# Gate projection of layers one and two as one rounded product over 80 stacked partitions

## The reference, cut to what matters

```python
h = x @ w_in                                   # (256, 2048) @ (2048, IN_WIDTH)
a_q, a_k, a_v, a_z, b_q, b_k, b_v, b_z, b_lr, m_q, m_z = jnp.split(h, cuts, axis=-1)
gate_logit = (b_lr @ gate_w + gate_b)          # b_lr: 256 x 16, gate_w: 16 x 256, per layer
log_g = jax.nn.log_sigmoid(gate_logit) / GATE_TAU
o_b = gla_chunk_recurrence(b_q, b_k, b_v, log_g)
```

## Time and profile before

| what | value |
|---|---|
| median of three executions | 2252.95 us (2252.88 to 2253.16) |
| span of the profiled execution | 2251.9 us |
| TensorE busy | 2240.0 us, 99% |
| TensorE weight loads | 2014.9 us, 89% |
| VectorE, ScalarE, GpSimd busy | 1555.0, 1296.2, 12.8 us |
| DMA | 460.04 MB, mean 204 GB/s |

### The profile page before, as it was taken

How to read it: one execution, slowest core, us unless ns; L and a number is a source line. 1 busy time by engine, 2 the same in 40 slices (tenths; PEclk the granted TensorE clock), 3 DMA queues, 4 the chain that set the end, 5 groups by cost and what they waited for, 6 DMA issues and landing times.

```text
span 2251.9 us, 35137 instructions
## 1 busy us (share of the span) xinstructions
PE 2240.0 (99%) x14045; PEld 2014.9 (89%) x14045; DVE 1555.0 (69%) x1772; ACT 1296.2 (58%) x1740; POOL 12.8 (1%) x18
## 2 busy tenths in 40 slices
PE   9999999999999999999999999999999999999998
PEld 8899998888999988888999999988999999998887
DVE  6576577775765777788787577866766666665555
ACT  6555576454555764666765467555655556554444
POOL 0000000000000000000000000000000000000000
PEclk9999999999999999999999999999999999999999
DMA  9655557676555684656565556675666666666664
GB/s 333 209 165 169 178 179 281 233 236 197 169 155 187 193 295 151 225 189 190 183 196 191 187 169 198 210 283 196 198 205 200 197 204 205 198 225 241 203 203 146
DMA packets 130532, 460.04 MB, mean 204 GB/s; under 512 B 13848, under 2 KB 20544, under 8 KB 128448
## 3 DMA queue, kind: packets, MB, share of 16 engines
q1 hardware_dynamic: 129376, 451.43, 60.8%
q0 software_dynamic: 848, 6.30, 0.8%
q10 hardware_dynamic: 144, 0.07, 0.0%
HBM read 449.35 MB, written 8.40 MB: 203 GB/s over the span
## 4 chain that ended last, share of the span: by engine, by line
PE 96%; DVE 2%; ACT 1%; DMA 1%; issue 0%; SPq 0%; DVEq 0%; ACTq 0%
PE banks L317 91%; PE banks L417 1%; PE banks L402 1%; PE banks L448 1%; PE banks L381 1%; PE banks L409 1%; DMA w_bc<-in_norm_mix_post 0%; DVE wl L652 0%; ACT wh L485 0%; DMA early<-in_kv_t 0%; PE banks L461 0%; PE banks L463 0%; PE banks L462 0%; DVE lacc L813 0%; PE banks L425 0%
## 5 line engine op out<-in xcount | busy, mean ns | idle before, releaser
L652 DVE TENSOR_TENSOR wl<-raw,wh 128x1024 fp32r<-128x1024 f32 x774 | 940.6, 1223 | 484.4 <-ACT wh L485 479.9
L485 ACT ACTIVATE wh<-raw 128x1024 fp32r<-128x1024 f32 (+1 forms) x777 | 813.2, 1052 | 494.5 <-PE banks L317 423.9
L317 PE MATMUL banks<-xx,wh 128*128 128x512 f32 (+1 forms) x3760 | 857.7, 380 | 0.0
L317 PEld LDWEIGHTS banks<-xx,wh 128*128 128x128 f32 (+1 forms) x3760 | 688.9, 189 | 91.6 <-issue 1.0
L317 PEld LDWEIGHTS banks<-xx,wl 128*128 128x128 f32 x3712 | 455.2, 192 | 13.5
L317 PE MATMUL banks<-xx,wl 128*128 128x256 f32 x3712 | 464.3, 276 | 0.0
L317 PE MATMUL banks<-wh,xx 128*128 128x512 f32 x1504 | 360.2, 380 | 0.0
L317 PEld LDWEIGHTS banks<-wh,xx 128*128 128x128 f32 x1504 | 282.9, 189 | 39.3
L317 PE MATMUL banks<-wl,xx 128*128 128x512 f32 x752 | 196.1, 379 | 0.0
L317 PEld LDWEIGHTS banks<-wl,xx 128*128 128x128 f32 x752 | 142.2, 189 | 20.1
L317 PE MATMUL banks<-wh,yy 128*128 128x512 f32 x416 | 98.4, 379 | 0.0
(11 more groups left out here) (287 smaller groups left out, 1762.7 us busy)
## 6 DMA issues: line engine op xcount, KB each, us to landing
raw<-in_w_in_f SPq DMA_DIRECT2D x304, 512.0 KB, 3.6
raw<-in_w_ffn_f SPq DMA_DIRECT2D x160, 512.0 KB, 4.0
raw<-in_w_ffn_down SPq DMA_DIRECT2D x88, 512.0 KB, 4.3
raw<-in_w_in_t SPq DMA_DIRECT2D x80, 512.0 KB, 3.6
raw<-in_w_out_t SPq DMA_DIRECT2D x64, 512.0 KB, 4.7
raw<-in_w_o_t SPq DMA_DIRECT2D x32, 512.0 KB, 4.7
raw<-in_kv_f SPq DMA_DIRECT2D x16, 512.0 KB, 3.9
raw<-in_w_up_a_f SPq DMA_DIRECT2D x16, 512.0 KB, 3.5
```

The lines of the kernel that those rows point to most:

```text
L317: return self.e.matmul(bank, stationary, moving, start=start, stop=stop, skip_group_check=True)
L485: self.e.activation(hi, source, ACT.Copy).then_inc(done.sem, 1)
L652: self.e.tensor_tensor(lo, source, hi.bitcast(f32), ALU.subtract).then_inc(done.sem, 1)
```

## The change

The gate projection is no longer a product of plain fp32. Weights and sums are split in a rounded part and a rest, and the parts are stacked on partitions, so that one rounded product of 80 rows and 256 columns gives, for each half, rounded times rounded, rest times rounded and rounded times rest. Rows 16 to 31 and 48 to 63 are zero.

The weights come in by one load of a table `gate_rows` (80 x 512), in which the weights of both layers stand three times, at partitions 0, 32 and 64, with zeros between. ScalarE rounds all 80 rows into `gw` and VectorE puts the rest into partitions 64 to 79, once. In each layer GpSimd clears `blr[0:80]`, then ScalarE writes the rounded sums to partitions 0 to 15 and 64 to 79 and VectorE the rest to 32 to 47. The sum itself now goes to a scratch `total`.

```diff
-        gw = sb("gw", 512)
+        gw = sb("gw", 512, f32r)
...
-                    i = self.e.matmul(banks[4][:, t * S:(t + 1) * S], gw[0:16, c:c + P], blr[0:16, :], start=True, stop=True)
+                    i = self.e.matmul(banks[4][:, t * S:(t + 1) * S], gw[0:80, c:c + P], blr[0:80, :], start=True, stop=True)
...
+            def gate_weights(self, graw, loaded, hi_done, lo_done):          # ScalarE
+                self.wait_ge(loaded)
+                self.e.activation(gw[0:80, :], graw[0:80, :], ACT.Copy).then_inc(hi_done.sem, 1)
+
+            def stack_gates(self, blr, total, made, cleared, free, hi_done, lo_done):
+                self.wait_ge(made, cleared, *free)
+                self.e.activation(blr[0:16, :], total, ACT.Copy).then_inc(hi_done[0].sem, 1)
+                self.e.activation(blr[64:80, :], total, ACT.Copy).then_inc(hi_done[1].sem, 1)
...
+            def gate_weights(self, graw, loaded, hi_done, lo_done):          # VectorE
+                self.wait_ge(hi_done)
+                self.e.tensor_tensor(gw[64:80, :], graw[64:80, :], gw[64:80, :].bitcast(f32), ALU.subtract).then_inc(lo_done.sem, 1)
+
+            def stack_gates(self, blr, total, made, cleared, free, hi_done, lo_done):
+                self.wait_ge(hi_done[0], cleared)
+                self.e.tensor_tensor(blr[32:48, :], total, blr[0:16, :].bitcast(f32), ALU.subtract).then_inc(lo_done.sem, 1)
...
+            def clear_gates(self, blr, free, done):                          # GpSimd
+                self.wait_ge(*free)
+                self.e.memset(blr[0:80, :].bitcast(f32), 0.0).then_inc(done.sem, 1)
...
-            t_gw = [load((l_gw0, l_gw1)[l_], gw[0:16, 256 * l_:256 * l_ + 256], A["b_gate_w"][l_]) for l_ in range(2)]
+            graw = at("graw", 104, 512)
+            t_gw = load(l_gw, graw[0:80, :], A["gate_rows"])
...
                 b, tok = narrow_f(X, free=x_ready)
-                c1 = narrow_sum(b, tok, 16, blr[0:16, :], tb[0:16, 0:S], fence + gate_free["t"])
+                total = tb[0:16, S:2 * S]
+                c1 = narrow_sum(b, tok, 16, total, tb[0:16, 0:S], fence + gate_free["t"])
+                cleared = after(sums_cleared)
+                x.clear_gates(blr, fence, cleared)
+                if l_ == 0:
+                    gates_hi, gates_lo = after(gates_rounded), after(gates_left)
+                    x.gate_weights(graw, t_gw, gates_hi, gates_lo)
+                sums_hi, sums_lo = afters(sums_rounded, 2), after(sums_left)
+                x.stack_gates(blr, total, c1, cleared, fence, sums_hi, sums_lo)
...
-                    made, free = (c1, t_gw[l_]), bank_free[4]
+                    made, free = (gates_hi, gates_lo, *sums_hi, sums_lo), bank_free[4]
```

More of the change, by code:

```diff
@@ L183 @@
         differences_across = evacuate = exact = exp_of_minus = exp_of_minus_abs = exps = first_product = \
-        forget_exps = forget_gates = forget_sum = gate_by = gate_half = gate_sum = gate_y = hi_features = \
+        forget_exps = forget_gates = forget_sum = gate_by = gate_half = gate_sum = gate_y = clear_gates = gate_weights = \
+        stack_gates = hi_features = \
         inverse_root = join = keep_awake = last_rows = level = linear_values = lo_features = load = \
@@ L229, in build @@
          decay_exped, offset_copied, o_copied, rms_made, exact_made, bounds_exped, ln_rooted, features_weighed,
-         squared, factor_made, z_scaled, columns_copied) = signals(
+         squared, factor_made, z_scaled, columns_copied, gates_rounded, sums_rounded) = signals(
             "act", "hi_made", "act_hi_made", "lo_copied", "act_evacuated", "narrow_copied", "act_activated", "exp_made",
             "weights_copied", "y_copied", "decay_exped", "offset_copied", "o_copied", "rms_made", "exact_made", "bounds_exped",
-            "ln_rooted", "features_weighed", "squared", "factor_made", "z_scaled", "columns_copied")
+            "ln_rooted", "features_weighed", "squared", "factor_made", "z_scaled", "columns_copied", "gates_rounded", "sums_rounded")
         (lo_made, act_lo_made, joined, dve_evacuated, narrow_added, soft_added, gated, scores_read, max_made, softmax_scaled,
@@ L236, in build @@
          layer_moments, layer_scaled, weights_multiplied, features_multiplied, row_copied, post_weighed, post_reduced,
-         post_added, product_made, asleep_cleared, keys_shifted) = signals(
+         post_added, product_made, asleep_cleared, keys_shifted, gates_left, sums_left) = signals(
             "dve", "lo_made", "act_lo_made", "joined", "dve_evacuated", "narrow_added", "soft_added", "gated", "scores_read",
@@ L241, in build @@
             "features_multiplied", "row_copied", "post_weighed", "post_reduced", "post_added", "product_made", "asleep_cleared",
-            "keys_shifted")
-        (bias_closed, scores_cleared, row_cleared, pool_added) = signals(
-            "pool", "bias_closed", "scores_cleared", "row_cleared", "pool_added")
+            "keys_shifted", "gates_left", "sums_left")
+        (bias_closed, scores_cleared, row_cleared, pool_added, sums_cleared) = signals(
+            "pool", "bias_closed", "scores_cleared", "row_cleared", "pool_added", "sums_cleared")
         NR, NH, NE, AHEAD = 5, 4, 6, 2
@@ L271, in build @@
         one_row = cst[:, 16 * P:17 * P]
-        l_const, l_vec, l_bias, l_res, l_st, l_bc, l_bc2, l_gw0, l_gw1, l_rows, l_keys0, l_keys1 = lines(
-            "l_const", "l_vec", "l_bias", "l_res", "l_st", "l_bc", "l_bc2", "l_gw0", "l_gw1", "l_rows", "l_keys0", "l_keys1")
+        l_const, l_vec, l_bias, l_res, l_st, l_bc, l_bc2, l_gw, l_rows, l_keys0, l_keys1 = lines(
+            "l_const", "l_vec", "l_bias", "l_res", "l_st", "l_bc", "l_bc2", "l_gw", "l_rows", "l_keys0", "l_keys1")
         l_out = lines(*(f"l_out{t}" for t in range(8)))
@@ L1623, in walk @@
             gq, gk, gv, gb = at("gq", 72, 512), at("gk", 74, 512), at("gv", 76, 1024), at("gb", 80, 512)
-            blr = at("blr", 82, S)
+            blr = at("blr", 82, S, f32r)
             li_mem = (at("le", 83, 512), at("lqe", 85, 512), at("lke", 87, 512), at("lacc", 89, 1536), at("lo", 95, 1024),
@@ L2562, in _ @@
             walk(Tensor(e))
-_DIRECT = ["b_gate_w", "ln_g", "ln_b", "norm_mix_post_2", "norm_ffn_post_2"]
+_DIRECT = ["ln_g", "ln_b", "norm_mix_post_2", "norm_ffn_post_2"]
 _WIDE = tuple(512 * n for n in range(4))
@@ L2592 @@
     arrays["memT"] = get["mem"][0].T
+    w, rows = _np.concatenate(list(get["b_gate_w"]), axis=1), _np.zeros((80, 512), _np.float32)
+    for k in (0, 32, 64):
+        rows[k:k + 16] = w
+    arrays["gate_rows"] = rows
     t = get["a_rel_bias"][:, :, ::-1]
```

## The result

| | median us | runs | profiled span us |
|---|---|---|---|
| before | 2252.93 | 2252.5 to 2253.35, 10 | 2251.9 |
| changed | 2257.57 | 2255.41 to 2261.29, 10 | 2259.5 |

The ratio is 1.0023, 95% interval 1.0015 to 1.0031: slower by 4.6 us, where 2.6 us were forecast. The median lies inside the range given. That the kernel is slower is clear; whether by more than the forecast's 0.2% is not, since 4.6 us are 0.21% and the interval begins at 0.15%. More telling than the median is the spread: 5.9 us, against 0.85 us before. (Beside the experiments the kernel before ran 59 more times: 2252.3 to 2254.6 us, but for one run at 2255.99 us. One more, at 2323.74 us and a mean clock of 0.948, fell in a slow state and is left out.) The profiled execution of the changed kernel is its slowest, at 2261.29 us, 1.8 us above its span.

The account below looks back on a forecast made before the run. TensorE, busy 99% of the span, was taken as the bound. Cheaper products (-2.06 us) and two waits with restarts (+4.6 us) made +2.57 us on 2252.95: 2255.5 us, range 2253.0 to 2258.0 us.

Parts of the forecast that it names:

- What bounds, and where the cost would be: TensorE bounds; at both layers' gate projections it waits for GpSimd's clearing of `blr`, queued behind the bias-table memset.
- The product: Gate projection on TensorE: two rounded products cost 0.22 us in place of 1.25, saving 1.03 us per layer.
- Wait of layer one: TensorE idles 2.56 us before layer one's gates, from 57.14 to 59.70 us; layer one ends +1.63 us.
- the bias table: Its load in layer one lands 0.34 us later behind the larger `gate_rows` load, moving GpSimd's memset to 58.02 us.
- The steps behind the memset: Layer one: clearing 0.33 us, ScalarE copy 0.37, VectorE subtraction 0.41, plus handing over; TensorE starts at 59.70 us.
- Wait of layer two: TensorE idles 1.88 us before layer two's gates, from 494.20 to 496.08 us; layer two ends +0.94 us.
- its last sentence: The prediction fails if the bias table lands at another time than before.
- The clock: Rival: TensorE's idle time at the gates halves its clock; one fall gives 2257.4 us, two 2259.3; chance 0.11.
- Backlog, loads, `bias_gates` at nothing: Delayed ScalarE and VectorE work, SyncE's loads and `bias_gates` behind the gates cost nothing; tightest margin 0.5 us.
- Not cheaper: Rival: the rounded 80-row product takes as long as before, losing 2.06 us: 2257.6 us; chance 0.02.
- no wait: Rival: the clearing is done before TensorE reaches the gates, winning 2.06 us: 2250.9 us; chance 0.10 including half wait.
- The tiling mode: Around the gate projection: 0.10 us on each side for changing to 16 rows and back goes with 80 rows.

Follow-up runs that it names:

- clear_first: The changed kernel with GpSimd's clearing of `blr` moved ahead of the bias-table memset (`close_bias`) on its queue; 2252.05 us, ratio 0.9997 to the kernel before.
- clear_first_early_load: As clear_first, with the load of `gate_rows` issued behind the constants, some 6 us earlier; 2251.36 us, ratio 0.9991 to the kernel before.
- second trace: Profile of the changed kernel run again unchanged, beside other experiments; 2258.28 us median, ratio 1.0020 to the kernel before.
- filled_wait: The changed kernel with ten unused products of 512 columns on TensorE just ahead of the gates' wait; 2256.55 us, ratio 1.0017 to the kernel before.
- sixteen_rows: As clear_first, but the product reads only the first 16 of 80 rows, without the rests; 2252.45 us, ratio 0.9998 to the kernel before.

## Why the prediction was wrong

- *What bounds, and where the cost would be:* right. Both places, the order of the chain, and who releases whom are as forecast, and `clear_first` shows that the order on GpSimd's queue is the cause.
- *The product:* right. Forecast 1.03 us saved per layer, measured 1.01.
- *Wait of layer one:* forecast 2.56 us, measured 3.34. The term mis-sized is the bias table. It was to be 0.34 us later, by 128 KB at 380 GB/s. From its issue to the memset it takes 6.9 us in the changed kernel, against 6.1 us before; in the seven traces with the large load ahead it lands 6.7 to 7.1 us after its issue, in two with the small loads 6.0 and 6.1, and in `clear_first_early_load`, with none of them just ahead, 6.4. So the load ahead goes with 0.3 to 1.1 us, where 0.34 was forecast; how much of it is the load and how much scatter, and why it would be more than its bytes, stays open. The steps behind the memset took 1.96 us in place of 1.68, mostly the last one: TensorE starts 0.25 us after VectorE's and ScalarE's rows end, 0.15 us in layer two, where 0.03 were put down.
- *Wait of layer two:* forecast 1.88 us, measured 2.57 in one trace and 1.30 in the other. The same table lands 7.7 and 6.5 us after its issue there, and 5.9 to 7.7 over all traces. Before the change nobody near waited for it, so this scatter did no harm; the change puts it on TensorE's path. The forecast took the one landing of the trace (7.3 us from issue to memset) as fixed; its last sentence names this as the way in which it would fail.
- *The clock:* this is the main step that failed; the two waits above are the smaller one. The sum has the clock at 1.00 throughout. Its fall was a rival with a chance of 0.11, on the ground that "the two forecast waits are just shorter than what the end shows". A granted clock below 1.00 near 60 us was one of its own signs of being wrong, and it is what both traces show. The idle times were longer than forecast, and the time from the last product to the fall at the program's end was no bound below which nothing happens: layer two fell with 2.57 us. The traces of this case have falls at idle times of 2.57, 2.83, 3.26, 3.34, 3.39 and 4.41 us, and none at 0.4 to 1.5 us. Of the Trainium skill, the page named in the prediction ("TensorE: Matmul & The Clock Gate", section "Why this matters for your kernels") was on the right side with its warning. The gaps that it warns of are longer than the 2.57 and 2.83 us that sufficed here; the measurement decides. The price was near the truth: 1.9 us forecast, measured 1.7 us each in the first trace. (The 1.9 us took the length of a row; a row reaches 0.16 us beyond the spacing of its products, as 1.89 against 1.73 us, so rows 11 give 1.7 as well.) The long fall in the second trace cost 3.1 us: 67.19 - 60.88 = 6.31 us for two rows that take 3.51, and 0.57 in place of 0.31 us for the gates.
- *What it makes together:* 2.57 us forecast, 4.6 and 4.9 us measured. How the 2 us between them divide is known only roughly. `filled_wait` has the same waits on GpSimd, no fall, and 3.6 us; without the 0.5 us that the filling costs in layer two that is 3.1 us. By this estimate the waits are half a microsecond to one longer than forecast, and the falls make 1.0 to 1.8 us of the median. The mean clock is 0.998 or less in 14 of the 21 executions, which suggests that most have a fall. The fastest, 2.0 and 2.5 us above the kernel before, come near the forecast's number, but none of them was traced: that they are what it describes is not shown. That the median lies inside the range is partly luck, as a fall in both layers alone was priced beyond its end (2259.3 us).
- *Backlog, loads, `bias_gates` at nothing:* right. No second wait follows in either trace. *Not cheaper, no wait:* both refuted. *The tiling mode:* the rule of the Trainium skill that was cited ("TensorEngine Tiling (Array Packing)", section Key Properties) fits the trace of `sixteen_rows`, which has 0.19 us on the two sides in layer two, as the forecast had 0.2 us, and another 0.19 us at the product itself. Its times don't show it.
- *Distance of time and span:* put at 1.05 us from the median. It is 1.8 to 1.9 us in every run whose span is listed, so the span of 2251.9 us belongs to an execution of about 2253.7 us and not to the median one; this moved nothing, as only the difference was used.

## What to carry to other kernels

Before a new wait is put on a queue, ask what stands ahead on the *producer's* queue: an engine that is busy for 1% of the time can still stand for 57 us ahead of one instruction that waits for a transfer. A chain through such an engine costs what of its length is not covered, holds every engine that waits for it, and brings the scatter of the transfer onto the path; if TensorE is to idle by it for as long as here, put a fall of the clock into the likeliest case and not among the rivals. Here a spread of runs that grew from about 1 to 6 us was the first sign of it.

## What the runs showed that was not expected

- Ten products without use (2.2 us) did not make the kernel slower. No fall of the clock is left in its trace, the spread shrank to 1.9 us, and the median is about 1 us nearer to the kernel before, though the intervals overlap.
- Two products with 16 rows in a stream of 128-row products cost 0.38 us more than two with 80 rows, in the trace of layer two.
- A fall of the clock lasted between 3 and 7 us and cost 1.7 to 3.1 us. The two long ones (idle times of 3.39 and 4.41 us) had begun before TensorE started again, the four short ones (2.57 to 3.34 us) within 1 us after it did. The length of the idle time alone does not separate them: 3.34 us was followed by a short fall and 3.39 us by a long one.
